# Latent attention in a 41,684-instruction hybrid stack: value products in a new order, values produced token-major

## What is computed

```python
q = (cq @ w_uq).reshape(b, s, 16, 128 + 64)            # nope and rope parts
w_uk, w_uv = w_ukv_h[..., :128], w_ukv_h[..., 128:]
scores = (q_nope @ k_nope^T + q_rope @ k_rope^T) * (128 + 64) ** -0.5
probs = softmax(scores)                                # non-causal, 512 x 512 per head
o = probs @ (ckv @ w_uv)                               # 512 x 128 per head
return o @ w_o
```

## Time and profile before

| | us |
|---|---|
| median of 3 runs | 2829.74 (2828.68 to 2835.11) |
| the profiled execution, own time | 2829.24 |
| its span in the trace | 2827.4 |
| PE busy | 2694.7 (95%) |
| DVE, ACT, POOL busy | 1397.5, 1209.3, 1075.5 |
| scores of the first pair to the end of the eighth | 2044.6 to about 2345 |

### The profile page before, as it was taken

One profiled execution on the slowest core, in us unless ns is written; L12 is line 12 of the kernel. 1 busy time (PEld: TensorE's weight loads), 2 busy tenths in 40 slices (PEclk: granted clock), 3 DMA queues, 4 the chain that ended last, 5 costly groups with the idle time before them and its releaser, 6 DMA issues.

```text
span 2827.4 us, 41684 instructions
## 1 busy us (share of the span) xinstructions
PE 2694.7 (95%) x13716; PEld 2128.3 (75%) x13716; DVE 1397.5 (49%) x2462; ACT 1209.3 (43%) x1879; POOL 1075.5 (38%) x803
## 2 busy tenths in 40 slices
PE   7999999899999899999999999999999999999998
PEld 6887777676767667778887788886667766788886
DVE  7335333776666567586755322138653443321126
ACT  5224433544444455365544333245554453432233
POOL 5544333432323332343334444444412213444442
PEclk9999999999999999999999999999999999999999
DMA  4333222211111222222222333332201102233331
GB/s 163 94 92 93 69 74 59 75 53 53 37 52 45 66 68 61 67 76 73 67 75 82 97 97 96 96 102 75 82 30 45 60 30 67 86 97 93 96 104 52
DMA packets 59639, 211.84 MB, mean 75 GB/s; under 512 B 6688, under 2 KB 7072, under 8 KB 59552
## 3 DMA queue, kind: packets, MB, share of 16 engines
q1 hardware_dynamic: 57744, 206.89, 24.0%
q10 hardware_dynamic: 1520, 2.75, 0.3%
q0 software_dynamic: 288, 1.05, 0.1%
HBM read 208.57 MB, written 2.10 MB: 75 GB/s over the span
## 4 chain that ended last, share of the span: by engine, by line
issue 38%; PE 36%; POOL 17%; DVE 7%; ACT 1%; DMA 0%; POOLq 0%; DVEq 0%; SPq 0%; ACTq 0%
POOL weights_low L371 17%; PE bank L1292 11%; PE bank L1294 10%; PE bank L1293 10%; DVE work L1728 1%; PE bank L1395 1%; PE bank L1061 1%; PE bank L1081 1%; DVE activations_low L451 1%; PE bank L1377 0%; DVE work L1725 0%; DVE work L965 0%; DVE work L963 0%; DVE to_split L676 0%; PE bank L1070 0%
## 5 line engine op out<-in xcount | busy, mean ns | idle before, releaser
L371 POOL TENSOR_TENSOR weights_low<-weights_raw,weights_high 128x512 fp32r<-128x512 f32 x776 | 1046.7, 1371 | 1599.4 <-ACT weights_high L355 1581.8
L1292 PE MATMUL bank<-activations_high,weights_high 128*128 128x512 f32 x2912 | 1185.3, 407 | 44.7 <-POOL weights_low L371 17.2
L1294 PE MATMUL bank<-activations_high,weights_low 128*128 128x512 f32 x2912 | 1141.6, 392 | 0.0
L1293 PE MATMUL bank<-activations_low,weights_high 128*128 128x512 f32 x2912 | 1140.7, 392 | 0.0
L1292 PEld LDWEIGHTS bank<-activations_high,weights_high 128*128 128x128 f32 x2912 | 550.1, 189 | 183.0 <-issue 20.7
L1294 PEld LDWEIGHTS bank<-activations_high,weights_low 128*128 128x128 f32 x2912 | 549.5, 189 | 117.3
L1293 PEld LDWEIGHTS bank<-activations_low,weights_high 128*128 128x128 f32 x2912 | 550.9, 189 | 110.7 <-issue 8.9
L355 ACT ACTIVATE weights_high<-weights_raw 128x1024 fp32r<-128x1024 f32 x384 | 403.9, 1053 | 300.7 <-PE bank L1294 293.1
L2818 DVE TENSOR_TENSOR mixed<-bank,mixed 128x512 f32 (+1 forms) x48 | 33.2, 692 | 193.9 <-PE bank L1294 193.9
L2762 ACT ACTIVATE to_split<-work 128x512 f32<-128x512 f32 x64 | 40.5, 632 | 184.0 <-DVE work L2804 184.0
L2804 DVE SCALAR_TENSOR_TENSOR work<-bank,rstd 128x512 f32<-128x512 f32 x64 | 44.2, 690 | 146.1 <-PE bank L1294 138.7
(11 more groups left out here) (439 smaller groups left out, 3135.0 us busy)
## 6 DMA issues: line engine op xcount, KB each, us to landing
weights_raw<-weights SPq DMA_DIRECT2D x388, 512.0 KB, 3.6
out_t<-residual SPq DMA_DIRECT2D x8, 256.0 KB, 2.0
residual<-x_t ACTq DMA_DIRECT2D x2, 512.0 KB, 7.4
residual<-x_t POOLq DMA_DIRECT2D x2, 512.0 KB, 9.9
work<-p_t ACTq DMA_DIRECT2D x2, 512.0 KB, 4.7
const<-consts SPq DMA_DIRECT2D x1, 713.0 KB, 12.6
const<-consts SPq DMA_DIRECT2D x1, 321.0 KB, 11.5
root<-positions ACTq DMA_DIRECT2D x1, 256.0 KB, 3.3
```

Source lines behind the costliest of these rows:

```text
L371: K.nc.gpsimd.tensor_tensor(K.w_lo[:, s, part], K.raw[:, s, part], K.w_hi[:, s, part].bitcast(F32), ALU.subtract).then_inc(K.job_sems["low ...
L1292: K.nc.tensor.matmul(dst, wh, K.act_hi[:, t, :], start=k == 0, stop=False)
L1293: K.nc.tensor.matmul(dst, wh, K.act_lo[:, t, :], start=False, stop=False)
L1294: ins = K.nc.tensor.matmul(dst, wl, K.act_hi[:, t, :], start=False, stop=k == len(tiles) - 1)
```

## The change

Three orders, one for each engine, take the place of two. The value job is written with the activations as the stationary operand and the weights of both heads as the moving one, so that its result is token-major: for each of four tiles of 128 tokens, six matmuls of 256 columns, two tiles per bank (tiles 2 and 3 in the ring's bank `v23`, tiles 0 and 1 in the job's). The transposes of the values and DVE's copies of them are gone. n1 is computed before n0, and n0's last matmul raises `jobs_done`. o0 stands ahead of t13; each o is done in two cuts, columns 0 to 383 once t{h}2 was read, columns 384 to 511 once t{h}3 was read.

```diff
-MLA_ORDER = ["n1", "k0", "k1", "v1", "s00", "s10", "s01", "vt0", "s11", "vt1", "t00", "t10", "s02", "s12",
-             "t01", "t11", "s03", "s13", "t02", "t12", "t03", "t13", "o0", "o1"]
+MLA_ORDER = ["n1", "k0", "k1", "v23", "s00", "s10", "s01", "s11", "t00", "s02", "t10", "s12", "s03",
+             "t01", "t11", "s13", "t02", "t12", "t03", "o0", "t13", "o1"]
+MLA_SCALAR_ORDER = ["s00", "s10", "s01", "s11", "t00", "t10", "s02", "s12", "t01", "s03",
+                    "t11", "t02", "s13", "t12", "t03", "o0", "t13", "o1"]
-MLA_VECTOR_ORDER = ["k0", "k1", "s00", "s10", "t00", "s01", "t10", "vt0", "s11", "t01", "vt1", "t11", "s02", "s12",
-                    "t02", "s03", "t12", "s13", "t03", "t13", "o0", "o1"]
+MLA_VECTOR_ORDER = ["k0", "k1", "s00", "s10", "t00", "s01", "s11", "t10", "t01", "s02", "t11", "s12", "s03",
+                    "t02", "t12", "t03", "s13", "t13", "o0", "o1"]
...
+def mla_values(e, c, bank, first):
+    K, mm, s = e.K, e.K.nc.tensor.matmul, c % SLOTS
+    wh, wl = (w[:, s, 4 * P:8 * P].rearrange("p (h a d) -> p a h d", h=2, a=2) for w in (K.w_hi, K.w_lo))
+    for t in (first, first + 1):
+        dst = bank[:, (t - first) * 2 * P:(t - first + 1) * 2 * P].rearrange("p (h d) -> p h d", h=2)
+        cut = slice(t * P, (t + 1) * P)
+        for a in range(2):
+            mm(dst, K.act_hi[:, 11 + a, cut], wh[:, a, :, :], start=a == 0, stop=False)
+            mm(dst, K.act_lo[:, 11 + a, cut], wh[:, a, :, :], start=False, stop=False)
+            ins = mm(dst, K.act_hi[:, 11 + a, cut], wl[:, a, :, :], start=False, stop=a == 1)
+    return ins
...
-    product(e, c, bank_of(e, c)[:, :], [8, 9, 10])
     ring.claim(f"n1_{s}", trip)
     ring.written(product(e, c, ring.bank(f"n1_{s}")[:, :], [8, 9, 10], 3))
-    ring.wait(f"n1_{s}", trip)
-    e.eng.sem_inc(K.job_sems["done"], 1)
+    product(e, c, bank_of(e, c)[:, :], [8, 9, 10]).then_inc(K.job_sems["done"], 1)
     job_start(e, c + 1, i)
-    for use, chunk0 in (("k0", 0), ("k1", 2), ("v1", 6)):
+    for use, chunk0 in (("k0", 0), ("k1", 2)):
...
-    product(e, c + 1, bank_of(e, c + 1)[:, :], [11, 12], 4).then_inc(K.job_sems["done"], 1)
+    ring.claim(f"v23_{s}", trip)
+    ring.written(mla_values(e, c + 1, ring.bank(f"v23_{s}"), 2))
+    mla_values(e, c + 1, bank_of(e, c + 1), 0).then_inc(K.job_sems["done"], 1)
...
-            ring.wait_read(f"t{h}3_{s}", trip)
-            if h == 0:
-                ring.wait_read(f"vt0_{s}", trip)
-            settle(e)
-            for t in range(QT):
-                ins = mm(dst[:, :], b.v_tok[h][:, t, :], b.pt[h][:, t, :], start=t == 0, stop=t == QT - 1)
+            for last, cut in ((2, slice(0, 3 * P)), (3, slice(3 * P, S))):
+                ring.wait_read(f"t{h}{last}_{s}", trip)
+                settle(e)
+                for t in range(QT):
+                    ins = mm(dst[:, cut], b.v_tok[:, t, h * P:(h + 1) * P], b.pt[h][:, t, cut],
+                             start=t == 0, stop=t == QT - 1)
```

More of the change, by code:

```diff
@@ L2967, in mla_uses @@
     return [f"{u}_{s}" for s in range(2) for u in MLA_ORDER]
[L2973 to L2977 removed]
+MLA_ORDER = ["n1", "k0", "k1", "v23", "s00", "s10", "s01", "s11", "t00", "s02", "t10", "s12", "s03",
[4 more added lines that the diff above has]
+                    "t02", "t12", "t03", "s13", "t13", "o0", "o1"]
 def mla_buffers(K):
     b = Names()
[L2982 removed]
+    (qr, v_tok, p, pt0, pt1) = carve(K, (DT, S), (QT, 2 * P), (2, S), (QT, S), (QT, S))
     mx, sums, rec = K.sinks[:, 0:4], K.sinks[:, 4:8], K.sinks[:, 8:12]
@@ L2989, in mla_buffers @@
     b.kn_lo, b.qn_hi, b.qn_lo = K.act_lo[:, free, :], K.y_r, K.act_hi[:, free, :]
-    b.kr_hi, b.kr_lo, b.v = K.rstd_r, K.act_lo[:, 2 * DT - 1, :], pt1[:, 0:2, :]
+    b.kr_hi, b.kr_lo = K.rstd_r, K.act_lo[:, 2 * DT - 1, :]
     b.qs = [K.root_r, K.act_hi[:, 2 * DT - 1, :]]
     b.p = [[p[:, 0, :], p[:, 1, :]], [K.sq[:, 0, :], K.sq[:, 1, :]]]
-    b.v_tok, b.pt = [v_tok0, v_tok1], [pt0, pt1]
+    b.v_tok, b.pt = v_tok, [pt0, pt1]
     b.stat = lambda a, h, q: a[:, 2 * h + q % 2:2 * h + q % 2 + 1]
@@ L2997, in mla_buffers, with mla_flat @@
     return b
+def mla_flat(v_tok, t):
+    return v_tok[:, t:t + 2, :].rearrange("p a d -> p (a d)")
 def mla_turned(b, t):
@@ L3093, in mla_pair_pe @@
             ins = mm(dst[:, :], b.qs[h][:, cut], b.kr_lo, start=False, stop=True)
[L3094 to L3098, removed]
-            settle(e)
-            for t in range(QT):
-                ins = nc.tensor.transpose(dst[:, t * P:(t + 1) * P], b.v[:, h, t * P:(t + 1) * P], ident)
         elif what[0] == "t":
@@ L3161, in mla_act @@
                 weight_high(e, c + AHEAD, i)
+                ring.wait(f"n1_{s}", trip)
+                act(b.qn_hi[:, 1, :], ring.bank(f"n1_{s}")[:, :], ACT.Copy, scale=scale).then_inc(K.sem("mla_high"), 1)
                 job_wait(e, c, i)
                 act(b.qn_hi[:, 0, :], bank_of(e, c)[:, :], ACT.Copy, scale=scale).then_inc(K.sem("mla_high"), 1)
-                ring.wait(f"n1_{s}", trip)
-                act(b.qn_hi[:, 1, :], ring.bank(f"n1_{s}")[:, :], ACT.Copy, scale=scale).then_inc(K.sem("mla_high"), 1)
                 turned = at(b.qr[part][s], i)
@@ L3173, in mla_act @@
                 weight_high(e, c + 1 + AHEAD, i)
-                use = f"v1_{s}"
+                use = f"v23_{s}"
                 ring.wait(use, trip)
-                ring.read(use, act(b.v[:, 1, :], ring.bank(use)[:, :], ACT.Copy))
+                ring.read(use, act(mla_flat(b.v_tok, 2), ring.bank(use)[:, :], ACT.Copy))
                 job_wait(e, c + 1, i)
[L3178 to L3181, removed]
+                act(mla_flat(b.v_tok, 0), bank_of(e, c + 1)[:, :], ACT.Copy).then_inc(K.job_sems["bank"][(c + 1) % SLOTS], 1)
+                for what in MLA_SCALAR_ORDER:
                     use, h, q = f"{what}_{s}", int(what[1]), int(what[-1])
@@ L3260, in mla_dve @@
                 e.eng.wait_ge(high, trip * 12 + s * 6 + 1)
+                ring.read(f"n1_{s}", v.scalar_tensor_tensor(b.qn_lo[:, 1, :], ring.bank(f"n1_{s}")[:, :], scale,
+                                                            b.qn_hi[:, 1, :].bitcast(F32), ALU.mult, ALU.subtract))
+                e.eng.wait_ge(high, trip * 12 + s * 6 + 2)
                 v.scalar_tensor_tensor(b.qn_lo[:, 0, :], bank_of(e, c)[:, :], scale, b.qn_hi[:, 0, :].bitcast(F32),
                                        ALU.mult, ALU.subtract).then_inc(K.job_sems["bank"][c % SLOTS], 1)
-                e.eng.wait_ge(high, trip * 12 + s * 6 + 2)
-                ring.read(f"n1_{s}", v.scalar_tensor_tensor(b.qn_lo[:, 1, :], ring.bank(f"n1_{s}")[:, :], scale,
-                                                            b.qn_hi[:, 1, :].bitcast(F32), ALU.mult, ALU.subtract))
                 turned = at(b.qr[part][s], i)
@@ L3278, in mla_dve @@
                                                        b.kn_hi[:, h, :].bitcast(F32), ALU.subtract))
-                    elif what[0] == "v":
-                        ring.wait(use, trip)
-                        ring.read(use, v.tensor_copy(b.v_tok[h], ring.bank(use)[:, :].rearrange("p (a d) -> p a d", d=P)))
                     elif what[0] == "s":
```

## The result

The changed kernel takes 2807.87 us (median of 4 runs, 2806.66 to 2810.84) against 2831.05 for the kernel before: ratio 0.9924, 95% interval 0.9912 to 0.9935. Forecast was 2808.5, a gain of 21.2 us; the ratio is one of 21.5. The ratios use fast runs alone; one slow execution of the kernel before, beside a later group of runs, took 3854.34 us at a mean granted clock of 0.654 and is left out of them.

A forecast was written before the change was run, and what follows sets the result against it. PE, busy 95% of the span, was taken as the bound. Sum: 8 x (-0.87 - 1.42 + 0.12) - 7 x 0.55 = -21.2 us from 2829.24, so 2808.0, stated as 2808.5; range 2803 to 2821.

The forecast's parts named there:

- (a): Value transposes removed from PE: -0.87 us a pair; two DVE copies of about 0.6 go too, called off the path.
- (b): Token-major values: 24 matmuls of 256 columns at 0.12 us replace 12 of 512 at 0.23: +0.12 a pair.
- Rivals A and C: Value matmuls take a load's 0.19 us, or load plus streaming, 0.305: 2822 or 2844 us; chances 0.12 and 0.02.
- (c): Between the two weight jobs: n1 before n0 removes PE's wait for its own matmul, -0.55 us in seven pairs.
- (d): New softmax order: PE's idle time falls from 2.27 to 0.85 us, -1.42 a pair.
- the hand schedule of the new order: Softmax start times worked out from s00: s13's exponential at 12.30 us, o0 at 13.22, waiting for that exponential.
- (e): Value products in two cuts, o0 ahead of t13: 0 us; bound +1.3 a pair.
- the cover for the late copy: Inside o0: t03's copy ends near 14.2 us, the first cut lasts to 15.8, covering the wait by 1.6.
- Rival B: Softmax hand-overs keep their gaps, idle 2.3 us a pair stays: 11.4 us less gain, 2820 us; chance 0.12.
- Rival D: Job gap is POOL's and softmax gaps stay: -6 us, or +7 with short matmuls load-bound; chance 0.06.
- four gaps of 2.33 less 0.02 each: PE's idle time within softmax, before s02, t03, t13 and o0; taken as 2.27 us a pair after start-up.
- rival A: Each 256-column value matmul costs a load's full 0.19 us: +1.80 a pair, 2822 us; chance 0.12.

The follow-up runs named there:

- old_orders_no_vt: Changed kernel with the three engine orders of before less value-transpose entries, o0 behind t13 and o uncut; token-major values and n1 first kept: 2812.71 us, ratio 0.9946.
- dve_load_kept: old_orders_no_vt plus two unneeded row maxima on DVE where it had copied the transposed values: 2819.77 us, ratio 0.9965.
- o_uncut: Changed kernel with each value product in one piece of 512 columns, waiting for the last copy of its head's transposes: 2824.95 us, ratio 0.9985.
- n1_first_alone: Kernel before with only n1 put before n0 on PE, ACT and DVE, n0's product raising jobs_done: 2824.69 us, ratio 0.9986.
- t02_bank_again: Second run of o0_on_t02_bank's kernel, beside the changed kernel again: 2801.92 us, ratio 0.9906.
- o0_after_t13: Changed kernel with o0 moved behind t13 on PE and ACT, both value products still in two cuts: 2812.02 us, ratio 0.9943.
- o0_on_t02_bank: Changed kernel with o0 claiming t02's bank and t13 that of s13, o0's first cut still ahead of t13: 2802.29 us, ratio 0.9905.

## Why the prediction was right, and where it was not

The period fell by 2.76 where 2.72 was forecast, the ratio is one of 21.5 us where 21.2 was; from the start of the first pair's s00 to that of the last the two profiles differ by 19.3 us, 7 x 2.76. By its steps:

- (a) and (b), the work: forecast 0.12 a value matmul, measured 0.12; with the -0.87 for the transposes that is -0.75, and it is what old_orders_no_vt leaves once its gap is taken off. Rivals A and C (0.19 and 0.3 each) fall with the rows; the Trainium skill's sentence that loads overlap only across row groups ("TensorE: Matmul & The Clock Gate", the section on packing) does not hold for these loads, which all use the full array and cost nothing beyond 0.12 a matmul; the one on the background weight buffer agrees with them.
- (c): the cause was right and the size too small: 0.69 measured for 0.55, short by 0.14 x 7 = 1 us.
- (d): the hand schedule of the new order is right to 0.15 us in each step, and names the right last wait. **The step that failed is its attribution.** It says that the new orders bring -1.42, and (a) calls the two copies on DVE "off the path". In old_orders_no_vt 0.75 of the 1.42 was there with the orders of before. It came with the token-major values, and needed two things that go with them: DVE without its copies (dve_load_kept: 0.84 us back for two operations of 0.6 in their places) and the ring without the transposes' two uses, so that s02 no longer claims s11's bank. The prediction has no word on the second. The new orders, o0's place and the cuts together brought 31.06 - 30.51 = 0.55. The sum held because the schedule had neither the copies nor the old ring in it: it was right on where the change ends, and it was luck that the split into parts did not matter.
- (e): 0 for the cut itself was near (o0 takes 0.11 more than forecast); the cover for the late copy was real and needed, as o_uncut shows.
- Rival B fell: there is one gap a pair, not four. Rival D fell with n1_first_alone.
- Small slips in the working changed nothing: four gaps of 2.33 less 0.02 each are 2.25 and not 2.27; by the schedule's own prices t12 has 0.33 us of slack and not at most 0.2; and rival A's time was 2822, just outside the range whose upper end it was to be.

## What to carry to other kernels

An operation on an engine that is half idle is not off the path if a hand-over stands behind it in that engine's queue: ask what is queued behind it and who waits for that, before it is costed at nothing. In a ring of buffers, look at which user's release each claim gets, again whenever a use is added or taken out, since every later claim moves. Here a claim on a buffer whose release is needed anyway removed the last 0.8 us of each pair, with no change of work. And where the profile's releaser contradicts the code, put the suspected wait back by itself: one line settled it.

## What the runs showed of the hardware that was not expected

The same kernel differs by some 4 us from run to run while its pair stage repeats to 0.04 us a pair. Part of it is the granted clock in other stages. These are windows of the same stretch, in the first profile of the changed kernel and in that of t02_bank_again (a row ends with the granted clock, the DMA share and GB/s):

```profile
2375.00:2425.00 50.00, 46.10 (x185) 36.71 (x184) 30.22 (x44) 25.71 (x38) 17.34 (x14) 0.93 0.24 70
```

```profile
2375.00:2425.00 50.00, 48.11 (x211) 39.02 (x210) 23.15 (x34) 25.09 (x35) 23.03 (x18) 1.00 0.28 85
```

The mean clock is 0.93 in the one and 1.00 in the other; the second profile of the changed kernel has 0.93 again. The stretch is the opening of the next stage, where PE stands idle in two places, for 2.0 and 1.9 us, in all 13 profiles of this case alike. In the first profile of the changed kernel the clock is at 0.51 for the 3.4 us behind the first of them, the lower of its two levels (1.2 and 2.4 GHz); in t02_bank_again it stays at 1.00 behind the same idle time:

```profile
2377.56 0.52 PE L1292 MATMUL bank<-activations_high,weights_high 128*128 128x512 f32 x1 [2.00 <-DVE activations_low L2317]
...
2378.30 0.63 PE L1294 MATMUL bank<-activations_high,weights_low 128*128 128x512 f32 x1
2378.72 0.63 PE L1292 MATMUL bank<-activations_high,weights_high 128*128 128x512 f32 x1
```

```profile
2378.00:2381.40 3.40, 3.40 (x10) 2.66 (x9) 3.40 (x7) 2.24 (x4) 0.00 (x0) 0.51 0.52 154
```

```profile
2368.22 0.50 PE L1292 MATMUL bank<-activations_high,weights_high 128*128 128x512 f32 x1 [2.01 <-DVE activations_low L2317]
2368.56 0.39 PE L1293 MATMUL bank<-activations_low,weights_high 128*128 128x512 f32 x1
2368.79 0.40 PE L1294 MATMUL bank<-activations_high,weights_low 128*128 128x512 f32 x1
```

```profile
2368.00:2372.00 4.00, 3.78 (x17) 3.13 (x18) 4.00 (x8) 2.18 (x4) 0.00 (x0) 1.00 0.44 131
```

Matmuls of 512 columns start 0.42 apart in the one and 0.23 in the other. Of the 13 profiles, eight show such a stretch behind one of the two idle times or behind both, and five (dve_load_kept, o0_after_t13, old_orders_no_vt and both of o0_on_t02_bank's version) behind neither.

One more such stretch, earlier and in code that no edit touches, is in the first profile of the changed kernel and not in the second:

```profile
1240.00:1250.00 10.00, 6.55 (x65) 5.46 (x64) 8.65 (x15) 5.86 (x7) 7.33 (x5) 0.83 0.49 148
```

```profile
1240.00:1250.00 10.00, 6.53 (x73) 5.43 (x72) 8.69 (x11) 6.90 (x9) 9.39 (x6) 1.00 0.54 157
```

With another one like it, near 1550 us, the first profile is 3.0 us behind that of the kernel before at 1990 us. The kernel before has one of its own near 2003 us, so at the first s00 the difference is down to 1.7.

What such a stretch costs shows best in o0_on_t02_bank and t02_bank_again, which are one kernel. Their profiled executions took 2802.79 and 2798.31 us, and all of the difference is there when the pairs begin: the first s00 starts at 2047.36 us in the one and at 2042.92 in the other. The first has the stretches near 1245 and 1550 us, and the second has neither. The same matmul starts 1.4 us later in the first at 1240 us, 2.9 later at 1260 and 4.5 later at 1580: about 1.5 us for each stretch. Of the rest, 1.2 us are there within the first 200 us of the program, and these were not traced.

What decides, from run to run, whether the clock falls behind such idle time is left open. So is whether it makes the 1.8 us by which t02_bank_again gained more than its pairs explain: nothing was tried, and the medians are of four and five executions of which one each was profiled.
